# A hybrid decoder layer on one core: the high and low halves of the memory probabilities packed into 32-bit words before they are transposed

## What is computed

```
def memory_attention(q_mem, mem_n, w_mem_kv):
    kv = mem_n @ w_mem_kv
    k_m, v_m = jnp.split(kv, 2, axis=-1)
    ...
    s = jnp.einsum('bthd,bmhd->bhtm', q, k_m) * (MEM_DH ** -0.5)
    p = jax.nn.softmax(s, axis=-1)
    o = jnp.einsum('bhtm,bmhd->bthd', p, v_m)
```

## Time and profile before

| | before |
|---|---|
| median of 3 executions | 1544.86 us (1543.43 to 1545.45) |
| span of the profiled execution, first to last instruction | 1543.8 us |
| PE matmul busy | 1443.0 us, 93% of the span |
| DVE, ACT, POOL busy | 724.0, 608.1, 236.4 us |
| mean granted TensorE clock over the span | 0.973 |
| one block in the loop | 87.8 us |

### The profile page before, as it was taken

How to read it: one execution, slowest core, us unless ns; L and a number is a source line. 1 busy time by engine, 2 the same in 40 slices (tenths; PEclk the granted TensorE clock), 3 DMA queues, 4 the chain that set the end, 5 groups by cost and what they waited for, 6 DMA issues and landing times.

```text
span 1543.8 us, 28261 instructions
## 1 busy us (share of the span) xinstructions
PE 1443.0 (93%) x11746; PEld 1046.2 (68%) x11746; DVE 724.0 (47%) x1221; ACT 608.1 (39%) x1101; POOL 236.4 (15%) x217
## 2 busy tenths in 40 slices
PE   3359699999999999999999999999999999999996
PEld 2238476776867677676867677686867767686762
DVE  2876625436172535527163544627163543616253
ACT  1344425344342534434252534434262534434241
POOL 1231201121110201121020202121020112112000
PEclk9669799999999999999999999999999999999998
DMA  8130100102010010102001010202001010201001
GB/s 337 65 136 1 42 2 28 54 0 82 0 69 12 27 54 10 71 0 82 0 36 46 27 54 0 82 0 82 0 27 54 21 61 0 82 0 46 10 28 68
DMA packets 15432, 69.32 MB, mean 45 GB/s; under 512 B 2352, under 2 KB 2480, under 8 KB 12848
## 3 DMA queue, kind: packets, MB, share of 16 engines
q1 hardware_dynamic: 15408, 68.98, 11.9%
HBM read 52.20 MB, written 16.78 MB: 45 GB/s over the span
## 4 chain that ended last, share of the span: by engine, by line
PE 90%; DVE 4%; ACT 2%; DMA 1%; issue 1%; POOL 1%; SPq 1%; DVEq 0%; ACTq 0%; POOLq 0%
PE bank L330 75%; PE bank L484 2%; PE bank L452 2%; PE bank L490 2%; PE bank L476 2%; PE bank L498 2%; DVE whl L852 1%; PE bank L541 1%; DVE wmx L816 1%; PE bank L463 1%; PE bank L388 1%; DMA whl<-in_pool_w 1%; PE bank L435 1%; PE bank L380 1%; POOL arena L1134 1%
## 5 line engine op out<-in xcount | busy, mean ns | idle before, releaser
L330 PE MATMUL bank<-arena,whl 128*128 128x256 f16 x6144 | 684.6, 274 | 2.6 <-DVE whl L852 2.6
L330 PEld LDWEIGHTS bank<-arena,whl 128*128 128x128 f16 x6144 | 602.3, 98 | 84.1 <-issue 6.5
L330 PE MATMUL bank<-arena 128*128 128x512 f16 x1536 | 344.1, 381 | 6.4 <-DVE arena L872 6.4
L330 PEld LDWEIGHTS bank<-arena 128*128 128x128 f16 x1536 | 147.8, 98 | 181.3 <-issue 15.4
L963 DVE SCALAR_TENSOR_TENSOR arena<-arena 64x256 f32<-64x256 f32 x60 | 25.2, 420 | 314.6 <-POOL arena L1191 313.2
L330 PE MATMUL bank<-whl,arena 128*128 128x512 f16 x768 | 168.3, 379 | 0.0
L686 ACT ACTIVATE arena<-bank,sca 128x512 f32<-128x512 f32 x64 | 43.9, 688 | 254.4 <-PE bank L330 253.3
L330 PEld LDWEIGHTS bank<-whl,arena 128*128 128x128 f16 x768 | 75.2, 99 | 86.9
L1143 POOL TENSOR_TENSOR arena<-arena 128x1024 f16<-128x1024 f32 x32 | 77.8, 2451 | 285.7 <-ACT arena L621 285.7
L1134 POOL TENSOR_TENSOR arena<-arena 128x1024 f32<-128x1024 f32 (+2 forms) x48 | 76.7, 1599 | 231.7 <-ACT arena L599 222.6
L1184 POOL TENSOR_TENSOR arena<-arena 128x542 f32<-128x542 f32 x16 | 17.4, 1090 | 606.1 <-ACT arena L693 598.3
(11 more groups left out here) (154 smaller groups left out, 1467.9 us busy)
## 6 DMA issues: line engine op xcount, KB each, us to landing
arena<-in_xt SPq DMA_DIRECT2D x16, 1024.0 KB, 5.2
arena<-in_x SPq DMA_DIRECT2D x32, 512.0 KB, 3.3
out<-arena SPq DMA_DIRECT2D x32, 512.0 KB, 2.6
arena<-in_w_in SPq DMA_DIRECT2D x8, 768.0 KB, 16.1
arena<-in_w_out SPq DMA_DIRECT2D x1, 4096.0 KB, 12.2
arena<-in_w_in SPq DMA_DIRECT2D x8, 392.0 KB, 16.2
arena<-in_w_mem SPq DMA_DIRECT2D x1, 2048.0 KB, 11.0
arena<-in_memt SPq DMA_DIRECT2D x1, 1024.0 KB, 6.6
```

Source lines behind the costliest of these rows:

```text
L330: mm = nc.tensor.matmul(ap, lhs, rhs, start=k == 0 and n == 0, stop=(k, n) == last)
```

## The change

The high and the low half of a probability are written into the two halves of one 32-bit word: `phl[..., h, 1::2]` is the high half and `phl[..., h, 0::2]` the low one. So ACT and DVE now write, and DVE reads, float16 elements at every second place. `pw` is the same memory seen as float32. `turn_p` transposes the words as float32: four 128x128 pieces instead of eight. The words land in PSUM as words, `pt_copy` still copies 1024 float16 elements (in four runs of 256 instead of eight runs of 128), and `pt` holds each token's low and high half side by side. The 24 matmuls read every second float16 element of it, `1 - b::2`.

The normalised probabilities are scaled by 2^14 (`PBITS`): `p_norm` multiplies the inverted sums by it in an instruction of its own, which waits for the inversion by a new semaphore `rs_inv`. The scale is taken out at L1087, where `o_vk` (`i_v` times 2^-14, computed once in the setup) stands for `i_v`.

```diff
-        phl = [view(O_T + 4096 + 2048 * b, [2, 2, NMEM], F16) for b in range(2)]
+        pw = [view(O_T + 4096 + 2048 * b, [2, NMEM], F32) for b in range(2)]
+        phl = [view(O_T + 4096 + 2048 * b, [2, 2 * NMEM], F16) for b in range(2)]
...
-        pt = view(O_XN, [NPAIR, 8, TB], F16)
+        pt = view(O_XN, [NPAIR, 4, 2 * TB], F16)
...
-                            for r in range(2):
-                                j = (h * MT + m) * 2 + r
-                                mm = nc.tensor.transpose(b16[b][:, j * P:(j + 1) * P],
-                                                         phl[n % 2][:, r, h, m * P:(m + 1) * P], ident16[:, :])
+                            j = h * MT + m
+                            mm = nc.tensor.transpose(bank[b][:, j * P:(j + 1) * P], pw[n % 2][:, h, m * P:(m + 1) * P],
+                                                     ident[:, :])
...
-                                                      vm[:, a, m, c:c + 64], pt[:, p, (h * MT + m) * 2 + b, :],
+                                                      vm[:, a, m, c:c + 64], pt[:, p, h * MT + m, 1 - b::2],
...
-                        a = nc.scalar.activation(phl[n % 2][:, 0, h, :], pr[n % 2][:, h, :], ACT.Copy,
+                        a = nc.scalar.activation(phl[n % 2][:, h, 1::2], pr[n % 2][:, h, :], ACT.Copy,
...
+            nc.vector.tensor_scalar(o_vk, i_v, 2.0 ** -PBITS, None, ALU.mult)
             nc.vector.tensor_scalar(gs, g_in, s_w, None, ALU.mult).then_inc(scaled, 1)
...
-                    nc.vector.reciprocal(rsum[:, 2 * n:2 * n + 2], psum_p[:, 2 * n:2 * n + 2]).then_inc(rs_ok, 1)
+                    nc.vector.reciprocal(rsum[:, 2 * n:2 * n + 2], psum_p[:, 2 * n:2 * n + 2]).then_inc(rs_inv, 1)
+                    dve.wait_ge(rs_inv, 4 * i + n + 1)
+                    nc.vector.tensor_scalar(rsum[:, 2 * n:2 * n + 2], rsum[:, 2 * n:2 * n + 2], 2.0 ** PBITS, None,
+                                            ALU.mult).then_inc(rs_ok, 1)
...
-                        a = nc.vector.scalar_tensor_tensor(phl[n % 2][:, 1, h, :], pr[n % 2][:, h, :],
-                                                           rsum[:, 2 * n + h:2 * n + h + 1], phl[n % 2][:, 0, h, :],
+                        a = nc.vector.scalar_tensor_tensor(phl[n % 2][:, h, 0::2], pr[n % 2][:, h, :],
+                                                           rsum[:, 2 * n + h:2 * n + h + 1], phl[n % 2][:, h, 1::2],
                                                            ALU.mult, ALU.subtract)
...
-                    nc.vector.tensor_copy(pt[:, p, :, t * P:(t + 1) * P],
-                                          b16[b].rearrange("p (a b) -> p a b", b=P)).then_inc(pt_out, 1)
+                    nc.vector.tensor_copy(pt[:, p, :, 2 * t * P:2 * (t + 1) * P],
+                                          b16[b].rearrange("p (a b) -> p a b", b=2 * P)).then_inc(pt_out, 1)
...
-                nc.vector.scalar_tensor_tensor(mixed[:, 6:8, :], bank[2][:, :].rearrange("p (a t) -> p a t", a=2), i_v,
+                nc.vector.scalar_tensor_tensor(mixed[:, 6:8, :], bank[2][:, :].rearrange("p (a t) -> p a t", a=2), o_vk,
```

More of the change, by code:

```diff
@@ L62 @@
 QBITS = 5 + XBITS + 5 + TOP + 1 - 15
+PBITS = 14
 MEM_AFTER = 5
@@ L98, in hybrid_block @@
         eps = sb("eps", [P, 2], F32)
-        sca = sb("sca", [P, 34], F32)
+        sca = sb("sca", [P, 36], F32)
         dec = sb("dec", [P, NPAIR, NC], F32)
@@ L180, in hybrid_block @@
         s_v, s_k, i_v, i_k = (col(n) for n in (22, 23, 24, 25))
-        sc_ms, sc_neg = col(30), col(31)
+        sc_ms, sc_neg, o_vk = col(30), col(31), col(34)
         gs = sca[:, 12:20]
@@ L212, in hybrid_block @@
                              "y_add", "y_ok"))
-        sT_ok, max_ok, nmax_ok, rs_ok, pn_ok, s_ok, pt_out, xn_ok, og_ok, mix_g, mix_m, mix_p, mmax_ok, m_sc, m_lo = (
-            sem(n) for n in ("sT_ok", "max_ok", "nmax_ok", "rs_ok", "pn_ok", "s_ok", "pt_out", "xn_ok", "og_ok",
+        sT_ok, max_ok, nmax_ok, rs_inv, rs_ok, s_ok, pt_out, xn_ok, og_ok, mix_g, mix_m, mix_p, mmax_ok, m_sc, m_lo = (
+            sem(n) for n in ("sT_ok", "max_ok", "nmax_ok", "rs_inv", "rs_ok", "s_ok", "pt_out", "xn_ok", "og_ok",
                              "mix_g", "mix_m", "mix_p", "mmax_ok", "m_sc", "m_lo"))
```

## The result

| | before | after |
|---|---|---|
| median of 16 executions each | 1544.53 us (1543.43 to 1546.47) | 1547.26 us (1545.85 to 1548.73) |
| ratio | | 1.0017, 95% interval 1.001 to 1.0024 |
| span of the profiled execution | 1543.8 us | 1547.3 us |
| PE, DVE, ACT, POOL busy | 1443.0, 724.0, 608.1, 236.4 us | 1444.7, 744.0, 611.9, 233.0 us |

The changed kernel is 2.7 us slower. That is inside the stated range, and just inside the 0.2% called "same", but it is a real loss: its interval leaves out 1. The forecast was 0.5 us less than the median known then (0.1 less than the one of 16 executions), and the likeliest case's own range ended at 1547. A profile shows one execution. That of the changed kernel took 1548.73 us, the longest of its 16, so the two spans differ by 3.5 us where the medians differ by 2.7.

What follows compares the result with a forecast made beforehand. PE was taken to bound the kernel, at 87.8 us a block in blocks 1 to 14. Terms -0.3 - 0.5 + 0 + 0.18 + 0.07 + 0.05 = -0.5 us, off the median 1544.86, gave 1544.4 us; range 1541 to 1552.

Steps and rivals of the forecast that it cites:

- the likeliest case: Whole kernel: no change, 1544.4 us with its own range 1542 to 1547, chance 0.78.
- The transposes: PE, each block: 16 float32 transposes (1.76 us) replace 32 float16 ones (1.78 us), 0.02 us less, 0.3 less in 16 blocks.
- The seam: PE, first L484 after the transposes: 0.95 us after float16, 0.89 after float32; half taken, -0.03 x 16 = -0.5 us.
- The 24 matmuls: PE, L541: reading every second float16 element costs 0, staying at 1.43 us; +1.18 us a block kept for the range.
- the two clocks a column of float32: PE, float32 matmuls: two clocks a column even at low clock, so taken as float32 arithmetic, not a read limit.
- The strided halves: ACT L738 and DVE L1013 writes at every second place: 0; upper bound 0.21 us per ACT, 0.26 per DVE instruction.
- The new multiply: DVE, `p_norm`: `rs_ok` comes 0.18 us later, four times a block; 0 in blocks 1 to 15, +0.18 in block 0.
- The cover: Quarters 1 and 2 of PE's output projection, blocks 1 to 15: hide the 0.18 us delay, 1.0 us spare before `turn_p(3)`.
- Block 0: First block, without output projection quarters: the inversion is on the chain once, so the added multiply costs +0.18 us.
- the rest: Setup and block 15: `o_vk` costs 0.07 us; block 15's tail nothing, at most 0.06 from float32 transposes' longer latency.
- the strided read: PE, 24 matmuls at float32 pace: 1.18 us a block, 17.7 us, 1562; chance 0.07 at full price, 0.05 at part.
- slower rival: Either L541 reading at float32 pace, 1562 us (0.07 full, 0.05 part), or doubled DVE and ACT half-word price, 1563 (0.03).

Runs made afterwards that it cites:

- the last experiment: Changed kernel with 32 useless setup matmuls, its DVE copy out of PSUM taking the words apart so the 24 matmuls read unit steps: 1560.67 us, ratio 1.0105.
- the padded runs: Useless matmuls added in the idle setup: kernel before with 96, 86, 82, 78: 1544.98, 1547.63, 1547.66, 1545.36 us; changed kernel with 32, 64: 1544.77, 1545.34 us.

## Why the prediction was wrong

**The transposes: right.** -0.02 us a block was forecast, -0.04 came (0.87 against 0.89 us, twice a block). The seam gave its whole 0.06, where half was taken. The central finding, that half as many float32 transposes cost the same, holds.

**The 24 matmuls: right in kind, sized too low.** Zero was taken between 0 and 1.18 us a block; 0.06 came, shown by itself in the run with unit steps. The argument that the two clocks a column of float32 are not the reach of the read is borne out: a float16 read over the same 4 bytes a column cost 4%, not 83%. The Trainium skill's rule on 16-byte lines ("SBUF — State Buffer", section "Door 1: The DMA port swizzle") is nearly right here: four hits in a line cost 4% on these matmuls and not nothing.

**The strided halves: sized too low.** The groups of the changed kernel, as in the earlier trace rows:

```profile
L1019 DVE SCALAR_TENSOR_TENSOR arena<-arena,rsum 128x256 f16<-128x256 f32 x128 | 64.0, 558 | 48.7 <-ACT arena L740 48.7
L740 ACT ACTIVATE arena<-arena,rsum 128x256 f16<-128x256 f32 x128 | 61.8, 568 | 28.7 <-DVE rsum L1012 28.7
L1012 DVE TENSOR_SCALAR rsum<-rsum 128x2 f32<-128x2 f32 x64 | 18.3, 287 | 2.2
```

ACT pays 568 against 498 ns for each write of a half, DVE 558 against 538. Zero was forecast for both. The new multiply takes 0.17 us as priced, but 0.67 where it falls beside a long POOL instruction (0.29 in the mean).

**The cover: right in its verdict, by less than thought.** `pt_copy(1)` ended 1.03 us before `turn_p(3)`; the shift was to take 0.18 of it. In the changed kernel, in the same block (start, us):

```profile
1227.56 0.68 DVE L1044 COPY arena<-bank 128x1024 f16<-128x1024 f16 x1
```

```profile
1228.21 1.04 PE L478 MATMUL bank<-ident,arena 128*128 128x128 f32 x8
```

The copy ends at 1228.24 and the second four of these eight begin at 1228.65: 0.41 us are left. The cover shrank by 0.6; the multiply and the longer writes of ACT and DVE are what is new ahead of it. PE still does not wait in the loop, but copies that are each 0.53 us longer were enough to break it, as the last experiment found. Block 0, which has no cover, took +0.42 us instead of +0.18 between these two profiles; in the padded runs it is 0.2, so its size is open.

**The step that failed** is the part called "the rest", where block 15 was given "nothing, and at most 0.06". It asked only how long the transposes take there, and not what else removing PE instructions changes: the place of all code behind them. The term that was missing is +2.4 us for one store, and a second one seems to hang on it. The last 48 matmuls (L330, now L333) wait for that store, and their chain piece is 0.6 us longer. The kernel before had

```profile
1513.29 12.81 PE bank L330 x48
```

against 13.41 in the changed one. Over these pieces the granted clock reads 0.82 before and 0.78 after; in its two idle stretches just ahead of them PE had stood 8.8 us, and now 11.1. In the profiles with a long store the 48 take 13.41, 13.09, 13.40 and 13.03 us at 0.78 to 0.80, and in one, the run with unit steps, 12.18 at 0.86; in the eight profiles without a long store they take 12.48 to 12.81 at 0.82 to 0.84. So a long store goes in four of five profiles with another 0.2 to 0.9 us at a lower clock, the fifth shows that it need not, and no run tests this by itself. With both terms the sum would have been, against the profiled span: -0.5 (loop), +0.4 (block 0), +2.4 (store), +0.6 (the 48), so +2.9, where the medians differ by 2.7 and the spans by 3.5. What is left of the spans is setup (+0.30; the first 32 matmuls took 6.70 us here, 6.47 before, and 5.35 to 6.45 in the experiments), which is not put down to the change.

That the time still fell inside the stated range is luck: the range had been stretched upward for the strided read, not for this.

**The rivals.** Neither slower rival happened at its price; the read stayed far below the 0.21 us a block from which it was to decide, and PE never waited for the copy in the loop. The result came on their side through a mechanism that was not on the list.

## What to carry to other kernels

Price a transpose by the distance between starts in a full series of its own type: four bytes a word at 0.110 us and two bytes at 0.056 make the packing worth nothing on PE, and what the packing adds (a multiply, strided halves, a strided operand) has to be paid out of that nothing. When code that runs once behind a loop stands on a chain of small DMAs, look at the instruction queue's packets there: here every edit that changed the number of PE's instructions ahead of them moved them. Before crediting or blaming an edit for as little as the 0.2% seen here, shift its code by some idle instructions and see whether the effect stays.

## What the hardware showed that was not expected

- A code load of 16 KB, 0.96 us long by itself, goes with a store of 512 KB that is 2.3 to 2.7 us longer when the late packets are a whole engine's share (stores of 5.06, 5.31, 4.96 and 5.13 us), 1.7 us when the load lies in between (4.32), and 0.2 us when it lies behind (2.81). In the packed records the late share starts, in all five long stores, where the code packet ends (1496.64 and 1496.65 us in the changed kernel), and its eight data packets (three with 86) then take 1.6 us (0.9). What is open is why the engine is not free earlier. The code packet itself lasts 1.93 us in the changed kernel; in the run without the scale it lasts 0.96, but is recorded only at 1496.0 us, 1.4 us behind the store's first packet, and the late share comes after it. So the engine may be held from the request for the code on. No run here tells the request apart from the transfer.
- A moving float16 operand at every second element costs 4% (1.49 against 1.43 us for 24 matmuls of 256 columns, two at a time).
- Float16 halves at every second element cost ACT 0.07 us for a write of 256 (498 to 568 ns) and DVE 0.02 us (538 to 558 ns) for reading one half and writing the other.
- A DVE copy of 1024 float16 elements out of PSUM that reads every second one takes 1.218 instead of 0.687 us. The Trainium skill, "Advanced Engine Details and Errata", section "VectorE Performance Modes", asks a unit step for the double rate; the step from 0.67 to 1.19 ns an element, each with the instruction's fixed part in it, goes that way, by a factor of 1.8.
